# Decay of a gated delta rule from broadcast rows and GpSimd masks instead of TensorE products

## What is computed

```python
gcum = jnp.cumsum(gc, axis=-1)
lower_incl = idx[:, None] >= idx[None, :]
decay = jnp.exp(jnp.where(lower_incl, gcum[..., :, None] - gcum[..., None, :], -jnp.inf))
l_mat = jnp.where(strict, jnp.einsum('bnhid,bnhjd->bnhij', kbeta, kc) * decay, 0.0)
...
qk = jnp.where(lower_incl, jnp.einsum('bnhid,bnhjd->bnhij', qc, kc) * decay, 0.0)
```

## Time and profile before

| | us |
|---|---|
| three runs | 1340.03, 1341.76, 1341.93 |
| median | 1341.76 |
| the profiled execution | 1343.92 |
| its span, first to last instruction | 1341.9 |
| mean granted TensorE clock | 0.975 of full |
| TensorE busy | 1266.5 (94%) |
| VectorE busy | 698.5 (52%) |
| ScalarE busy | 411.1 (31%) |
| GpSimd busy | 148.7 (11%) |

### The profile page before, as it was taken

The page is one execution under the profiler, slowest core; times in us unless marked ns, Lnnn a source line. Parts: engine busy times, 40 slices in busy tenths (PEclk is TensorE's granted clock), DMA queues, the critical chain, the costliest instruction groups (busy, mean ns, idle before and its releaser), DMA issues.

```text
span 1341.9 us, 17346 instructions
## 1 busy us (share of the span) xinstructions
PE 1266.5 (94%) x6360; PEld 1071.1 (80%) x6360; DVE 698.5 (52%) x1068; ACT 411.1 (31%) x754; POOL 148.7 (11%) x184
## 2 busy tenths in 40 slices
PE   5999999994899999888999999999999999999997
PEld 4888878883788888767888888888888888888875
DVE  5332444644766666626536354545545454535457
ACT  5221233643345555224321212121212222121222
POOL 1221001300133333113000000000000000000005
PEclk9999999996899999988999999999999999999999
DMA  7321323444233331122111010101010101010033
GB/s 245 133 86 52 92 86 99 149 138 140 78 102 104 105 105 47 62 96 95 64 62 63 31 63 31 63 31 63 31 63 31 63 31 63 31 63 31 32 126 126
DMA packets 90698, 106.52 MB, mean 79 GB/s; under 512 B 17407, under 2 KB 75551, under 8 KB 90655
## 3 DMA queue, kind: packets, MB, share of 16 engines
q1 hardware_dynamic: 90655, 105.96, 24.1%
HBM read 82.84 MB, written 23.10 MB: 79 GB/s over the span
## 4 chain that ended last, share of the span: by engine, by line
PE 51%; POOL 1%; issue 1%; DVE 1%; ACT 0%; POOLq 0%
PE f_ps_up L2265 12%; PE f_ps_up L2266 12%; PE f_ps_up L2267 12%; PE sums L2276 5%; PE sums L2278 5%; PE sums L2277 5%; POOL stage L1985 1%; POOL f_conv L1985 0%; DVE split L2190 0%; POOL f_stat L2249 0%; DVE f_w_lo L2124 0%; ACT f_w_hi L2056 0%; POOLq L1890 0%; DVE f_conv L2203 0%; DVE h_t L2183 0%
## 5 line engine op out<-in xcount | busy, mean ns | idle before, releaser
L2265 PE MATMUL f_ps_up<-split,f_w_hi 128*128 128x512 f32 x704 | 275.7, 392 | 3.2 <-DVE split L2190 3.2
L2266 PE MATMUL f_ps_up<-split,f_w_hi 128*128 128x512 f32 x704 | 275.1, 391 | 0.0
L2267 PE MATMUL f_ps_up<-split,f_w_lo 128*128 128x512 f32 x704 | 275.1, 391 | 0.0
L2129 DVE SCALAR_TENSOR_TENSOR f_conv<-f_ps_up,f_taps,f_conv 128x1023 f32<-128x1023 f32 x88 | 112.8, 1282 | 275.0 <-ACT f_conv L2060 269.5
L2265 PEld LDWEIGHTS f_ps_up<-split,f_w_hi 128*128 128x128 f32 x704 | 132.9, 189 | 31.8 <-DVE f_w_lo L2124 2.3
L2267 PEld LDWEIGHTS f_ps_up<-split,f_w_lo 128*128 128x128 f32 x704 | 132.9, 189 | 27.8
L2266 PEld LDWEIGHTS f_ps_up<-split,f_w_hi 128*128 128x128 f32 x704 | 133.0, 189 | 27.4
L2060 ACT ACTIVATE f_conv<-f_ps_up,f_taps 128x1024 f32<-128x1024 f32 x44 | 53.2, 1208 | 326.1 <-PE f_ps_up L2267 326.1
L2141 DVE TENSOR_TENSOR h_t<-sums,h_t 128x512 f32<-128x512 f32 x168 | 111.1, 686 | 39.8 <-PE sums L2278 39.7
L2276 PE MATMUL sums<-f_w_hi,f_y_hi 128*128 128x512 f32 x320 | 124.6, 389 | 0.0
L2277 PE MATMUL sums<-f_w_lo,f_y_hi 128*128 128x512 f32 x320 | 124.5, 389 | 0.0
(11 more groups left out here) (293 smaller groups left out, 2071.2 us busy)
## 6 DMA issues: line engine op xcount, KB each, us to landing
stage<-in_w_up SPq DMA_DIRECT2D x22, 1024.0 KB, 5.1
stage<-in_w_down SPq DMA_DIRECT2D x11, 1024.0 KB, 4.9
x_tile<-in_x SPq DMA_DIRECT2D x12, 512.0 KB, 4.3
stage<-in_w_in SPq DMA_DIRECT2D x6, 1024.0 KB, 6.6
qkv<-conv SPq DMA_DIRECT2D x11, 512.0 KB, 3.5
rows<-p_row SPq DMA_DIRECT2D x8, 644.0 KB, 3.2
stage<-rows SPq DMA_DIRECT2D x8, 644.0 KB, 4.1
stage<-in_w_in SPq DMA_DIRECT2D x8, 512.0 KB, 5.5
```

The lines of the kernel that those rows point to most:

```text
L2129: op = dve.scalar_tensor_tensor(conv[:, q, k:S], ps_up[:, q % 2, 0:S - k], taps[:, bass.ds(ct + (FTAPS - 1 - k) * 2 * FT, 1)], conv[:, q, ...
L2265: pe.matmul(bank, hi, h_hi[:, k, cols], start=(k == 0), stop=False)
L2266: pe.matmul(bank, hi, h_lo[:, k, cols], start=False, stop=False)
L2267: op = pe.matmul(bank, lo, h_hi[:, k, cols], start=False, stop=(k == KD - 1))
```

## The change

The cumulated gates are turned once, unsplit, and written to a DRAM scratch `cum` of 32 rows by 128. In `mix_block` a new DMA, `load_cum(u)`, reads the four rows of tile u with a broadcast to all 128 partitions into `row_cum` (256 KB written). GpSimd adds the two masks (`a_cum(u, C_DEC)` into `dec`, `a_cum(u, C_DECT)` into `dec_t`), and ScalarE takes the exponential in place, from SBUF. `a_decay` is gone from TensorE, and with it the waits of `a_trl` and `a_trinv` for `dec_set`. The negated sinks move from DVE to GpSimd.

```diff
+            sp.wait_ge(s_gv, 11)
+            sp.dma_start(io["cum"].rearrange("(r s) -> r s", s=P), cum_rows).then_inc(s_tab, 16)
             sp.wait_ge(s_tab, 96)
...
+            def load_cum(u):
+                ready((cum_set, u - 1, C_DECT))
+                src = io["cum"][bass.ds(reg(u * (H * P)), H * P)].unsqueeze(0).broadcast_to([P, H * P])
+                sp.dma_start(flat(row_cum[:]), src).then_inc(cum_in.sem, 16)
...
                 if n:
                     load_qkv(t + 2, par)
                     load_v(t + 2, par)
+                    load_cum(t + 2)
                 if d:
                     load_x(t - 1)
...
-            def a_cum(u):
-                after(pool, front, u - 1, F_DECT)
-                own = own_rows[:, bass.ds(u, 1)].rearrange("p t h -> p (t h)")
-                pool.tensor_tensor(row_cum[:], cum_rows[:].bitcast(F32).unsqueeze(1).broadcast_to([P, H, P]), over_cols(own),
-                                   ALU.mult).then_inc(cum_set.sem, 1)
+            def a_cum(u, n):
+                after(pool, cum_in, u)
+                if n == C_DEC:
+                    after(pool, low_set, u - 1)
+                else:
+                    after(pool, qk_set, u - 1)
+                out, mask = ((dec, M_LOW), (dec_t, M_TRI))[n - 1]
+                pool.tensor_tensor(out[:], row_cum[:], over_heads(masks[:, mask]), ALU.add).then_inc(cum_set.sem, 1)
...
                 if n:
-                    a_cum(t + 2)
+                    a_cum(t + 2, C_DEC)
                 if e:
                     d_rstd(t - 2, 2)
...
                 if n:
                     a_gates(t + 2, par)
+                    a_cum(t + 2, C_DECT)
                     a_rnorm(t + 2, par)
...
-            def a_decay(u, which):
-                if which == F_DEC:
-                    after(pe, cum_set, u)
-                    if not (isinstance(u, int) and u == 0):
-                        after(pe, q_n2, u)
-                else:
-                    after(pe, dec_set, u, 1)
-                    after(pe, turned, u - 1, 1)
-                far = exact[:, LOW_R if which == F_DEC else TRI_R].unsqueeze(1).broadcast_to([P, H, P])
-                pe.matmul(bank("a1"), exact[:, ONES_R], row_cum[:], start=True, stop=False)
-                pe.matmul(bank("a1"), exact[:, ID_R], far, start=False, stop=True).then_inc(front.sem, 1)
```

More of the change, by code:

```diff
@@ L92 @@
 I_CUM, I_NCUM, I_BETA, I_NBETA, I_OUT, I_IN, I_LAST = range(NG)
-ONES_R, ID_R, LOW_R, TRI_R = range(4)
+M_ONES, M_LOW, M_TRI = range(3)
 class Kept:
@@ L251, in project @@
         spare = lambda a, n: h[:, a:a + n]
[L252 to L256, removed]
+        tri, strict, ones = (spare(n * P, P) for n in range(3))
+        g_tmp = spare(5 * P, 6 * T * H).rearrange("p (n t h) -> p n t h", n=6, h=H)
+        g_log = spare(5 * P + 6 * T * H, T * H).rearrange("p (t h) -> p t h", h=H)
+        ab = spare(4 * P + T * H, 2 * T * H).rearrange("p (t c h) -> p t c h", c=2, h=H)
         convrows = spare(7 * P, P)[0:GTAPS * A_TILES]
         a_log, dt_bias, a_exp = (sb(n, [P, H]) for n in ("a_log", "dt_bias", "a_exp"))
-        gates, cum_rows, exact = kept.gates, kept.cum_rows, kept.exact
+        gates, masks = kept.gates, kept.masks
+        cum_flat, cum_rows = spare(3 * P, T * H), spare(3 * P + T * H, P)[0:T * H]
+        io["cum"] = nc.dram_tensor("cum", (T * H * P,), F32, kind="Internal").ap()
         ps_t = ctx.enter_context(nc.psum_tensor("ps_t", [P, 2, HALF], F32))
@@ L409, in _ @@
             tiles(pool, tile)
[L410 to L417, removed]
+            pool.wait_ge(s_tab, 80)
+            pool.tensor_copy(masks[:, M_ONES], ones).then_inc(s_zero, 1)
+            pool.tensor_scalar(masks[:, M_LOW], tri, FAR, None, ALU.mult).then_inc(s_zero, 1)
+            pool.tensor_scalar(masks[:, M_TRI], strict, -FAR, None, ALU.mult).then_inc(s_zero, 1)
         @block.scalar
@@ L582, in _ @@
             gv(dve.tensor_tensor(g_tmp[:, 4], sums[:, 1], gates[:, :, I_CUM], ALU.subtract))
[L583 to L587, removed]
+            gv(dve.tensor_copy(cum_flat.rearrange("p (t h) -> p t h", h=H), gates[:, :, I_CUM]))
             conv_rest(dve, kept, 2, 0)
@@ L653, in _ @@
             both(2, 0)
-            pe.wait_ge(s_gv, 13)
-            pe.transpose(cum_turned, cum_sums, ident).then_inc(s_ps_g, 1)
+            pe.wait_ge(s_gv, 10)
+            pe.transpose(cum_turned, cum_flat, ident).then_inc(s_ps_g, 1)
             both(2, 1)
@@ L766, in mix_block @@
         E_KTR, E_NORM = 1, 2
-        front = tally("front", 5)
-        F_DEC, F_DECT, F_KK, F_TRL, F_KQ = range(1, 6)
+        front = tally("front", 3)
+        F_KK, F_TRL, F_KQ = range(1, 4)
+        C_DEC, C_DECT = 1, 2
         vtr = tally("vtr")
@@ L937, in _ @@
             load_first(H, 2 * H, s_first_k)
+            load_cum(0)
             load_v(0, 0)
@@ L954, in _ @@
             load_blk(0)
+            load_cum(1)
             load_row(1)
@@ L1079, in _ @@
             a_gates(0, 0)
-            a_cum(0)
+            a_cum(0, C_DEC)
+            a_cum(0, C_DECT)
             a_rnorm(0, 0)
@@ L1083, in _ @@
             pool.wait_ge(s_load, LOADS)
+            pool.tensor_scalar(neg_sinks[:], sinks[:], -1.0, None, ALU.mult).then_inc(s_zero, 1)
             b_zw(0, 0)
             c_kprev(0, 0)
-            a_cum(1)
+            a_cum(1, C_DEC)
             a_rq(0, 0)
@@ L1090, in _ @@
             a_rq(1, 1)
+            a_cum(1, C_DECT)
             def step(t, par, n, a, b, d, e):
@@ L1140, in a_dec @@
                 after(act, gs_set, u)
-                after(act, front, u, F_DEC)
-                after(act, low_set, u - 1)
+                after(act, cum_set, u, C_DEC)
                 for h in range(H):
-                    op = act.activation(dec[:, h], bank("a1")[:, h], ACT.Exp, bias=gs[:, par, I_CUM, h:h + 1], scale=-1.0)
+                    op = act.activation(dec[:, h], dec[:, h], ACT.Exp, bias=gs[:, par, I_CUM, h:h + 1], scale=-1.0)
                 op.then_inc(dec_set.sem, 1)
             def a_dect(u, par):
-                after(act, front, u, F_DECT)
-                after(act, qk_set, u - 1)
+                after(act, cum_set, u, C_DECT)
                 for h in range(H):
-                    op = act.activation(dec_t[:, h], bank("a1")[:, h], ACT.Exp, bias=gs[:, par, I_NCUM, h:h + 1], scale=1.0)
+                    op = act.activation(dec_t[:, h], dec_t[:, h], ACT.Exp, bias=gs[:, par, I_NCUM, h:h + 1], scale=1.0)
                 op.then_inc(dec_set.sem, 1)
@@ L1584, in a_norms @@
                 for h in range(H):
-                    op = pe.matmul(ps["a1"][:, h:h + 1], squares[:, h], exact[:, ONES_R, 0:1].bitcast(F32), start=True, stop=True)
+                    op = pe.matmul(ps["a1"][:, h:h + 1], squares[:, h], masks[:, M_ONES, 0:1], start=True, stop=True)
                 op.then_inc(early.sem, 1)
@@ L1636, in a_trl @@
                 after(pe, low_set, u)
-                after(pe, dec_set, u, 2)
                 after(pe, bv_set, u - 1)
@@ L1675, in a_trinv @@
                 after(pe, added, t, NTH[n])
-                if a:
-                    after(pe, dec_set, t + 1, NTH[n])
+                if n == FIRST and a:
+                    after(pe, q_n2, t + 1)
                 elif n == FIRST:
```

32 lines of the change are left out of this document (11 added, 21 removed).

## The result

| us | before | after |
|---|---|---|
| median | 1341.28 (4 runs) | 1387.93 (4 runs, 1386.24 to 1391.49) |
| the profiled execution | 1343.92 | 1386.86 |
| its span | 1341.9 | 1385.1 |

The changed kernel is 1.035 times as long, 95% interval 1.033 to 1.037: 46.6 us slower, where 27 were forecast and 37 stood at the end of the range. The granted clock fell only from 0.975 to 0.967 of full.

A forecast was written before the change was run, and what follows sets the result against it. VectorE was taken to pace each step from `a_low` to `c_trp(1)`, TensorE the rest. 1341.8 - 5.0 (products) + 25.6 (wait) + 6.8 (clock) = 1369 us, range 1355 to 1379.

The forecast's parts named there:

- The new wait: Steps 2 to 5: GpSimd's add waiting for `load_cum` delays `d_rstd`, making `d_norm` 6.4 us late each; 25.6 us lost.
- the absorbers: Slack before `c_trp(1)`: 3.3 us at `c_scores(1)`, 1.1 at `d_tr2`, none at `c_trp(1)`; so all 6.4 us arrive.
- The clock: Steps 2 to 5: TensorE's idleness lowers its clock at `c_trp(1)`, one low stretch per step; 6.8 us lost.
- the rival with the clock up: Same delay in steps 2 to 5, but idleness doesn't lower the clock at `c_trp(1)`: 1362 us; chance 0.22.
- the rival with the clock down: Clock stays low through most of TensorE's half of steps 2 to 5, 16 us in all: 1378 us; chance 0.12.
- The products that go: Sixteen pairs of TensorE products removed, two per tile; 9 pairs count at 0.55 us each: 5.0 us gained.
- The first pair: In a steady step, before `a_inv(4)`: it covers the wait for VectorE's mask, so its removal is worth nothing.
- The second pair: In a steady step, before `a_inv(5)`, whose mask is already done: removal gains the whole 0.55 us.
- the new adds: Two 128x512 GpSimd adds per tile, 1.27 us by the nearest row: hidden, as GpSimd is busy 11 of 35 us.
- `project` and the start: Store of `cum` in `project`, `load_cum(0)` and first adds at the start of `mix_block`: zero, 1 us either way.

The follow-up runs named there:

- The exchange: Changed kernel with two GpSimd statements swapped, the second `d_rstd` ahead of the add into `m_dec` that waits for `load_cum`: 1364.6 us.
- a_all_0: Changed kernel with 384 bytes of padding ahead of all tiles and 128 ahead of the network's, so weights and streamed operands stand at 0 modulo 512: 1373.1 us.
- a_swap_pad: Changed kernel with both repairs, the second `d_rstd` ahead of the add into `m_dec` and the 640 bytes per partition put back: 1343.5 us.
- a_front: Both repairs on the changed kernel (`d_rstd` ahead of the add, 640 bytes back), plus `load_cum(0)` and `load_cum(1)` issued later and `a_rnorm(0)` before the first adds: 1341.0 us.
- a_kept_pad: Changed kernel with the 640 bytes per partition put back where the two removed tiles stood, ahead of all that moved: 1367.6 us.
- a_ffn_384: Changed kernel with 384 bytes per partition of padding ahead of the network's tiles: 1367.9 us.
- a_ffn_192: Changed kernel with 192 bytes of padding ahead of the network's tiles: 1382.2 us.
- b_ffn_pad: Kernel before the change with 1408 bytes per partition of padding ahead of the network's tiles: 1359.5 us.

## Why the prediction was wrong, point by point

*The new wait: right.* Forecast were a landing 4.2 us after the issue (427.7 to 431.9), `d_norm` 6.4 us late, and all of it passed on to `c_trp(1)`. Measured in step 3: 4.2, 6.4 and 6.1 us. Over the four steps `d_norm` was 24.5 us late where 25.6 were forecast, and 23.8 of them arrived at `c_trp(1)`: the absorbers were as small as read. The exchange took 24.4 us from the loop, in which are also the clock's 1.8, below, and against it 1.2 us that the adds then cost. The estimate of 2.6 us for 256 KB, by the Trainium skill's "DMA: Bandwidth & Descriptors" (Anatomy of one DMA), would have put the landing 1.6 us too early.

*The clock: mis-sized.* Four low stretches at 1.7 us each, 6.8 in all, were added. In step 3 the granted clock was 1.00 throughout although TensorE was idle for 2.70, 1.81 and 1.82 us. Only step 4, where it was idle for 2.20, 1.98 and 1.13 us, has a low stretch at that place (0.50 is 1.2 GHz); its windows:

```profile
493.00:496.00 3.00, 1.78 (x8) 1.46 (x8) 2.81 (x8) 1.66 (x11) 0.20 (x1) 0.73 0.46 103
496.00:499.00 3.00, 1.87 (x8) 1.63 (x8) 1.61 (x3) 2.85 (x12) 2.72 (x4) 0.50 0.30 89
499.00:502.00 3.00, 3.00 (x16) 2.51 (x14) 0.56 (x3) 0.89 (x5) 0.00 (x0) 0.64 0.00 0
```

TensorE's half of step 4 took 16.37 us, those of the other three 14.54 to 14.64: the low stretch costs 1.8 us, about the 1.7 that were taken for one. Step 2 had low clock too, 0.50 throughout 406 to 412 us, but inside the vector engine's half, where it cost nothing: 6.5 us of delay went in and 6.3 came out. So the term was some 2 us, not 6.8, and the rival with the clock up was nearer. Ten kernels have the wait, with 40 such steps. TensorE's half took 14.5 to 14.6 us in 31 of them, 16.1 to 16.4 in six and 19.3 in three: the rival with the clock down exists, but is rare. In one of the three, in `a_all_0`, TensorE had waited 5.48 us before `c_scores(1)`, and some 10 us of its half ran at half clock:

```profile
417.00:420.00 3.00, 3.00 (x14) 2.70 (x14) 0.74 (x5) 1.35 (x9) 0.00 (x0) 0.50 0.00 0
420.00:423.00 3.00, 3.00 (x12) 2.81 (x13) 1.39 (x6) 0.00 (x0) 2.65 (x4) 0.50 0.00 0
423.00:426.00 3.00, 3.00 (x12) 2.61 (x12) 0.14 (x1) 1.29 (x3) 0.71 (x2) 0.50 0.00 0
```

Its step took 48.9 us, 4.8 of it for the clock; the vector engine's half was 3 us longer than in the changed kernel's step 3, because there the load was issued and landed later.

*The products that go: right in mechanism, a little too large.* 5.0 us were to come back, 0.55 a step in the loop. TensorE's half of a step is shorter by 0.43 to 0.47 us, in the changed kernel (outside step 4) as in those with the repairs. The first pair is worth nothing, as forecast: `a_inv(4)` starts 1.84 us after `a_off(4)` with the pair (447.96 to 449.80) and without it (462.63 to 464.47). The second pair is worth 0.47: from `c_trk` to `d_tr` it is 0.22 us (467.69 to 467.91) where it was 0.69 (453.03 to 453.72), because `c_trk` itself had only 0.14 us to its successor while the pair stood there (453.03 to 453.17). The rows of before, then of after (`a_off` L1657 and L1647, `c_trk` L1731 and L1721, the pair L1608, `d_tr` L1767 and L1757):

```profile
447.96 1.06 PE L1657 MATMUL m_ps_a<-m_inv,m_low_t 128*128 128x128 f32 x8
...
453.03 0.38 PE L1731 MATMUL m_ps_c<-table,m_k_dup 128*128 128x128 f32 x2
453.17 0.47 PE L1608 MATMUL m_ps_a<-m_row_cum,exact 128*128 128x512 f32 x1
...
453.72 0.60 PE L1767 MATMUL sums<-table,m_mix_a 128*128 128x128 f32 x4
```

```profile
462.63 1.06 PE L1647 MATMUL m_ps_a<-m_inv,m_low_t 128*128 128x128 f32 x8
...
467.69 0.38 PE L1721 MATMUL m_ps_c<-table,m_k_dup 128*128 128x128 f32 x2
467.91 0.60 PE L1757 MATMUL sums<-table,m_mix_a 128*128 128x128 f32 x4
```

What the five pairs outside these four steps are worth, 2.8 of the 5.0 us, no run isolates. That *the new adds* are hidden was wrong as a rule and right only by luck: in the changed kernel the add into `m_dec` runs while the vector engine is idle for its sake. As soon as the wait was repaired it cost: the vector engine's half of the four steps was 1.3 us longer in `a_swap_pad` and 2.8 in `a_front`, where the pairs give 1.9. I had read that GpSimd is busy 11 of 35 us, and not what the vector engine does at that moment.

*`project` and the start: missed by 3 us.* Zero was forecast, with 1 us either way. Step 2 came 3.2 us late (383.08 to 386.25). 1.2 of it arose before the mixer's first product, which is hardly more than chance: nine kernels with this `project` at these addresses started the mixer between 234.2 and 236.1 us, before did at 234.3, and the addresses explain some 0.8. The other 2.0 arose in the start of the mixer. From its first product to the copy of step 2 it is 148.1 and 148.8 us in the two kernels with the old start, and 148.6 to 154.0, 150.8 in the mean, in the twelve with the new one. The broadcast load stands ahead of others, and these land later. DMA issues from 225 to 262 us, before, then after (count, KB each, median us to landing):

```profile
stage<-rows SPq DMA_DIRECT2D x2, 644.0 KB, 4.5
```

```profile
stage<-rows SPq DMA_DIRECT2D x2, 644.0 KB, 6.0
```

In the changed kernel TensorE waits 1.18 us for the first of them, where it did not wait before. I had costed the queue position in the loop and not at the start. That this load makes the whole 2 us is not shown: `a_front`, which moves it, gives back 1.4 us of the start of the mixer in one profile, within that spread.

*The step that failed: the network.* There was no term for it at all. The prediction took what the diff leaves alone to cost what it cost, and the diff removes two tiles from the front of the memory. That was worth 17.1 us in the network and about 1 in `project`, two fifths of the loss, and it is the distance from the forecast: measured are 3.2 (start) + 23.6 (loop) - 0.6 (steps 6, 7 and the end of the mixer) + 17.1 = 43.3 us, rounded, of the 43.2 by which the span grew, where the forecast had 0 + 30.2 - 2.8 + 0 = 27.4. The medians differ by 3.4 more than the spans: the profiled execution of before was 2.6 above its median and that of after 1.1 below, and 0.3 less lies outside its span. Without the addresses, `a_kept_pad`, the change gives 1367.6 us. That the forecast of 1369 came so near to this is in part luck: the span of `a_kept_pad` is longer than that of before by 2.1 (start) + 24.6 (loop) - 2.4 (the rest), so a clock term 5 us too large stood against a start 2 us too small.

## What to carry to other kernels

When a change adds or removes a tile, list the addresses of every tile behind it and compare, for each large product, the weights' with the streamed operand's; padding of a few hundred bytes is a cheap and telling control experiment. A wait for a DMA goes behind everything on its queue that somebody needs sooner, at the start of the program too. And work that is "hidden" on an idle engine has to be laid beside what the other engines do at that moment, not beside its busy share.

## What the runs showed of the hardware

The pace of back-to-back products of 128x512 in float32r, each with its own weights, depends on where the two operands lie: 0.2267 us when their addresses agree modulo 256 bytes (products into `f_ps_up`, kernel before, `a_ffn_384`, `a_all_0`), 0.233 when they differ by 64 or 128 (changed kernel, `a_ffn_192`, `b_ffn_pad`), nearly 3% more with TensorE busy all the time and the granted clock at 1.00. Differences other than 0, 64, 128 and 256 bytes were not tried, nor other shapes and types. The cause inside the chip is open. I did not expect it, and the Trainium skill speaks against it: by "SBUF — State Buffer" (Who interferes with whom) the two reads of TensorE, weights and moving operand, go through independent ports, and PE never waits on anyone. The measurement decides here. It would fit a conflict between just these two reads, since moving both (`a_all_0`) is free and moving one is not. But that is not shown: in the changed kernel the product of `f_w_lo` and `f_y_hi`, which agree, was slow beside one whose operands differ, and no run looked at the loads of weights apart.
